# Norms, gating and turning dealt into the seven-product stages, gate rows into routing, skip term begun in the projection

## The reference, cut to what matters

```
layer 0: h = modulate(rms_norm(x)); o = gated_delta(h);
         o = rms_norm(o per head of 128) * silu(h @ w_z);  x += gate * (o @ w_out)
layer 1: y = ssd(h) + d_skip * xs;  y = rms_norm(y * silu(h @ w_z)) @ w_out;  x += gate * y
both:    h = modulate(rms_norm(x)); route each token (softmax, top-k per expert);
         x += gate * experts(h)
then x = rms_norm(x, final_norm_g), and twice:
         m = mixer(rms_norm(x, mix_pre));  x += rms_norm(m, mix_post)
         f = swiglu(rms_norm(x, ffn_pre)); x += rms_norm(f, ffn_post)
```

## Time and profile before

| | us |
|---|---|
| median of 3 runs (4990.16 to 4994.88) | 4993.59 |
| the profiled execution's own time | 4995.03 |
| its span in the profile | 4993.3 |
| PE busy, of the span | 4098.9 (82%) |
| DVE busy | 2111.5 (42%) |
| ACT busy | 806.3 (16%) |
| POOL busy | 444.8 (9%) |
| mean granted clock of PE, share of full speed | 0.912 |

### The profile page before, as it was taken

How to read it: one execution, slowest core, us unless ns; L and a number is a source line. 1 busy time by engine, 2 the same in 40 slices (tenths; PEclk the granted TensorE clock), 3 DMA queues, 4 the chain that set the end, 5 groups by cost and what they waited for, 6 DMA issues and landing times. The chain is left out here.

```text
span 4993.3 us, 71953 instructions
## 1 busy us (share of the span) xinstructions
PE 4098.9 (82%) x30734; PEld 2813.9 (56%) x30734; DVE 2111.5 (42%) x3566; ACT 806.3 (16%) x1757; POOL 444.8 (9%) x486
## 2 busy tenths in 40 slices
PE   4988988876599996998887847775876999797997
PEld 2577658755244444585586622222355887446876
DVE  1655555554422212274474531110334445464445
ACT  1322232200000001152251000000121000151000
POOL 0012002200011110040040001110000000000000
PEclk7999999988799997989898969998987999898999
DMA  4500230002599991100101259999011222112221
GB/s 164 183 21 2 95 126 2 2 18 109 211 385 388 385 378 62 37 15 30 38 1 68 77 224 391 391 393 365 19 51 38 75 78 93 55 68 72 85 80 51
DMA packets 237213, 664.83 MB, mean 133 GB/s; under 512 B 15122, under 2 KB 32479, under 8 KB 236895
## 3 DMA queue, kind: packets, MB, share of 16 engines
q1 hardware_dynamic: 222302, 639.25, 34.0%
q0 software_dynamic: 14592, 20.98, 2.0%
HBM read 637.12 MB, written 23.07 MB: 132 GB/s over the span
## 5 line engine op out<-in xcount | busy, mean ns | idle before, releaser
L603 PE MATMUL bank<-hT_b,weight_ring 128*128 128x384 f32 x1792 | 592.7, 491 | 17.9 <-PEq L178 17.3
L603 PEld LDWEIGHTS bank<-hT_b,weight_ring 128*128 128x128 f32 x1792 | 339.5, 191 | 265.5 <-issue 41.8
L2292 PE MATMUL bank<-weight_ring,xs_b 128*32 128x512 f32 x2640 | 317.9, 634 | 64.5 <-DMA weight_ring<-in_moe_w_up 58.3
L2292 PE MATMUL bank<-weight_ring_extra_b,xs_b 128*32 128x512 f32 x2480 | 278.7, 600 | 29.2 <-DMA weight_ring_extra_b<-in_moe_w_up 29.2
L1477 PE MATMUL bank<-mixed_b,swiglu_sums_b 128*128 128x256 f32 x1056 | 239.5, 384 | 5.8 <-DVE swiglu_sums_b L1524 5.8
L2292 PEld LDWEIGHTS bank<-weight_ring,xs_b 128*32 128x32 f32 x2640 | 84.3, 116 | 272.7 <-issue 184.0
L1477 PEld LDWEIGHTS bank<-mixed_b,swiglu_sums_b 128*128 128x128 f32 x1056 | 203.5, 193 | 34.9 <-issue 6.5
L2360 DVE TENSOR_SCALAR xs_b<-bank,factor_b,mod_b 128x64 f32<-128x64 f32 (+1 forms) x384 | 95.4, 323 | 296.9 <-PE bank L2275 296.9
L2292 PEld LDWEIGHTS bank<-weight_ring_extra_b,xs_b 128*32 128x32 f32 x2480 | 79.2, 110 | 207.0 <-issue 178.5
L2261 POOL DMA_INDIRECT residual<-moe_out_b,slot_row_parts x80 | 123.9, 1549 | 725.8 <-DVE moe_out_b L2374 711.1
L2349 ACT ACTIVATE moe_silu_b<-bank 128x256 f32<-128x256 f32 x80 | 25.5, 383 | 1003.9 <-PE bank L2292 1003.9
(11 more groups left out here) (491 smaller groups left out, 7593.2 us busy)
## 6 DMA issues: line engine op xcount, KB each, us to landing
weight_ring_extra_b<-in_moe_w_down SPq DMA_DIRECT2D x34, 2048.0 KB, 25.5
weight_ring<-in_moe_w_gate SPq DMA_DIRECT2D x66, 1024.0 KB, 16.8
weight_ring<-in_moe_w_up SPq DMA_DIRECT2D x66, 1024.0 KB, 20.2
weight_ring_extra_b<-in_moe_w_gate SPq DMA_DIRECT2D x62, 1024.0 KB, 17.8
weight_ring_extra_b<-in_moe_w_up SPq DMA_DIRECT2D x62, 1024.0 KB, 18.9
weight_ring<-in_moe_w_down SPq DMA_DIRECT2D x30, 2048.0 KB, 23.6
weight_ring<-in_ada_w SPq DMA_DIRECT2D x24, 2048.0 KB, 7.9
weight_ring<-in_ssd_w_in SPq DMA_DIRECT2D x12, 2048.0 KB, 8.0
```

The source lines that it names most:

```text
L603: last = pe.matmul(acc, w[:, k, c * P:(c + 1) * P], hT[:, k, h * half:(h + 1) * half], start=(k == 0), stop=(k == KT - 1))
L2292: last = pe.matmul(in_bank(g)[lanes[c], :], xs[:, e % 2, kt, g * GROUP:(g + 1) * GROUP], w[:, k, :, c * COLS:(c + 1) * COLS], start=(kt == 0),
```

## The change

`gemm_seven` gets two hooks. `heads` deals the head norms, gating, turning and the spreading of the gate rows into the z products (`DeltaHeads` in layer 0, `BlockHeads` in layer 1); `tail` deals what follows an out product into its last units and behind them (`RouteTail`, `JoinTail`, both through `Renorm`). `norm_rows` takes the place of `load_x` + `norm_turn` and works in groups of two rows, each with its own load. `gate_rows`, `norm_turn`, `load_x`, `add_normed`, `final_norm`, `head_norm`, `rms_rows`, `turn_all` and `store` are gone. Buffers `heads_out`, `X`, `mixed`, `hT` live longer, so that rows stay in SBUF: only `x_dram` and `h_dram`, which the expert stage reads, are still written. In layer 1 rows are turned unscaled, and their inverse root comes in the out product's evacuation. The core of it:

```
 gemm_seven, SP:
+    tail.load(sp); ring.feed(sp, loads[-2][2])
+    for g in range(pairs - 1): tail.store(sp, steps, g)
     ring.feed(sp, last_load)
+    tail.store(sp, steps, pairs - 1); tail.end(sp, pairs)
 gemm_seven, PE:
     (unit 0, plain)
+    heads.spread_gate(pe)
+    u == 1: heads.wait_gate(pe)
+    u >= LAG (3): heads.turn(pe, u - LAG, u % 2, (3, 0))     # 8 transposes, banks 3 and 0 of this unit
+    before products 4 and 1: heads.wait_turned(pe, u - LAG, ...)
     (all units done)
+    for g in range(pairs): steps.turn(pe, g, g - 1 if 0 < g < pairs - 1 else None)
+    heads: turn the last three units (after combined of the last but one)
 gemm_seven, ACT:
+    heads.start_scalar(act, 0)            # layer 0: 24 squares of 128 columns with sums
     evacuate unit 0
+    heads.copy_gate(act); heads.start_scalar(act, 1)          # 24 more
     for u in range(1, len(units)):
+        heads.move_on_scalar(act, u - LAG, ...)
+        evacuate(act, u - 1)              # was behind the copy of the first product
+        heads.on_scalar(act, u - 2)       # layer 1: 2 squares of 512 columns
         copy of the first product
+        g = u - u0                        # u0: first unit of the last load
+        g >= 1: pre_square(g - 1), pre_root(g - 1)
+        M and g >= 0: post_square(g), post_root(g)
+        g >= 1: scale_on_scalar(g - 1)
+    for g in range(pairs - 1): move_on_scalar(g)
+    pre_square, pre_root, scale_on_scalar, move_on_scalar (pairs - 1)
 gemm_seven, DVE, for each u:
     combine(u), evacuate(u)
+    heads.on_vector(dve, u - 1)           # layer 0: 2 x 4 ops of 128 columns; layer 1: 2 of 512
+    g >= 1: pre_inverse(g - 1), scale_on_vector(g - 1)
+    M and g >= 0: post_inverse(g), join(g)
+ behind the units: move_on_vector(0 .. pairs - 2), pre_inverse, scale, move (pairs - 1)

+Renorm: a group is two rows of 1024.
+    square: ACT.Square with accum_out, each waits for the one before
+    mean (DVE) -> root (ACT) -> inverse (DVE); row 0 of a group scaled by ACT, row 1 by DVE
+    join: per row scalar_tensor_tensor (times inverse, times gain), then tensor_tensor (X += M)
+    turn: 8 transposes a row into two banks
+    move: bank 0 by ACT, 4 ops of 128 columns; bank 1 by DVE, 4 ops of 128 with a shift,
+          one of 512 without
 norm_rows:
-    load_x: one DMA of all rows, wait; norm_turn over all rows
+    one DMA for each row, a semaphore for each group; ACT: pre_square(g + 1) before scale(g),
+    move(g - 1) behind it; DVE: pre_inverse(g), scale(g), move(g - 1)
 route:
+    PE, behind the turning of the affinities: for each 512 columns of gate rows 4 spreads;
+    ACT copies them, behind Exp
 conv_project, "turn" jobs of the SSD, before the copy:
+    skip: Y[t, pair] = x * d, one tensor_tensor of 128 columns for each of 4 tiles
 ssd_scan:
-    if s < other: dve.tensor_copy(y, ...)
-    else: wait; dve.tensor_tensor(y, y, ..., ADD)
+    if s >= other: wait
+    dve.tensor_tensor(y, y, ..., ADD)
-    vector_ops: x *= skip; y += x          # after each half of the scan
 layer 1 out product, evacuation:
-    add_gated: tmp = part * gate;           X += tmp
+    add_scaled: tmp = part * inverse * gate; X += tmp
 RouteTail: X rows loaded at the start of the out product; per group the rows are stored to
+    x_dram, the normed rows to h_dram; in layer 0 groups 0 and 1 are normed in place, behind
+    the store of the same rows. The turned rows lie in heads_out, which route reads.
```

More of the change, by code:

```diff
@@ L405, in _ @@
         @block.sync
         def _(sp):
[L407 to L450, removed]
+            for g in range(G):
+                for target, source in sources(g):
+                    sp.dma_start(target, source).then_inc(loaded[g], 16)
@@ L454, in _ @@
         def _(act):
[L455 to L459, removed]
+            if gain is not None:
+                for g in range(G):
+                    steps.post_square(act, g)
+                    steps.post_root(act, g)
+            steps.pre_square(act, 0)
@@ L465, in _ @@
[L465 to L480, removed]
+            if gain is not None:
+                dve.wait_ge(gain_loaded, 16)
+                for g in range(G):
+                    steps.post_inverse(dve, g)
+                    steps.join(dve, g)
@@ L482, in _ @@
+            for g in range(G):
+                steps.pre_inverse(dve, g)
+                steps.scale_on_vector(dve, g)
+                if g:
+                    steps.move_on_vector(dve, g - 1)
+            steps.move_on_vector(dve, G - 1)
         @block.tensor
         def _(pe):
[L484 to L496, removed]
@@ L499, in input_parts @@
[L499 to L510, removed]
-            for target, part in parts:
-                sp.dma_start(target, part).then_inc(loaded, 16)
-            sp.wait_ge(loaded, 16 * len(parts))
+            for g in range(G):
+                steps.turn(pe, g, g - 2 if g >= 2 else None)
@@ L1226, in gemm_seven, with rows_ready, tail_bank @@
         first = core.sb(own, "first_product", 2, 1, HN)
+        def rows_ready(engine, g, q):
+            engine.wait_ge(moved, 2 * (u0 + g) + q + 1)
+        def tail_bank(g, q, i):
+            return core.bank[4 * ((u0 + max(g, pairs - 2)) % 2) + 2 * q + i]
+        row_groups = [[tiles[p], tiles[p + pairs]] for p in range(pairs)]
+        steps = tail.steps(core, own, tail_sems, row_groups, rows_ready, tail_bank) if tail else None
+        turns = steps is not None and steps.hT is not None
+        if heads:
+            heads.begin(own, tail_sems, [[tiles[p], tiles[p + pairs]] for _, p in units], [loads[i][0] for i, _ in units],
+                        moved, combined)
         def tokens(i):
@@ L1254, in _ @@
         def _(sp):
+            if tail:
+                tail.load(sp)
+                ring.feed(sp, loads[-2][2])
+                for g in range(pairs - 1):
+                    tail.store(sp, steps, g)
             ring.feed(sp, last_load)
+            if tail:
+                tail.store(sp, steps, pairs - 1)
+                tail.end(sp, pairs)
         @block.tensor
@@ L2807, in first_norm @@
     hT = core.sb(own, "hT", KT, T)
+    groups = [[t, t + 1] for t in range(0, TT, 2)]
     with ExitStack() as inner:
@@ L2914, in ssd_layer @@
+        inv = core.sb(own, "ssd_inverse", TX)
+        gate = core.sb(own, "gate", 1, D)
         yT = core.sb(own, "ssd_yT", SI // P, NX)
[L2915 to L2916 removed]
+        with ExitStack() as sums:
+            heads = BlockHeads(core, sums, inv[:], kept.rearrange("p (t n) -> p t n", t=TX), yT[:], gate[:])
+            gemm_seven(core, hT[:, :, NC:], [[(f"ssd_z{j}", KT)] for j in range(SI // 512)], range(TC, TT),
+                       heads.evacuate, "ssd_z3", block_sums(core, sums), on_scalar=True, heads=heads)
```

795 lines of the change are left out of this document (558 added, 237 removed).

## The result

The changed kernel takes 4732.4 us (median of 4 runs, 4728.4 to 4738.2) against 4993.1 before: a ratio of 0.948, with 95% interval 0.946 to 0.950. The forecast was 4741, with a range of 4700 to 4790. PE is busy 86% of it, ACT 20% (it was 16%), DVE 43%, and the mean granted clock rose from 0.912 to 0.935.

The account below looks back on a forecast made before the run. PE bounds the products; between them PE stands nearly still while a chain runs through one engine at a time. Gains summing to 252.3 us take the profiled 4995.0 to 4742.7, median 4741, range 4700 to 4790.

Parts of the forecast that it names:

- Products with heads: Layers' z products: head norm, gating, turning and gate rows dealt in; 92.4 against 127.4 and 122.0 against 150.6 us.
- Routing tails: Behind the out products of layers 0 and 1: 21.9 against 59.4 and 19.5 against 45.5 us.
- Join tails: Behind ev_out and od_out 18.5 us, gains 17.1 and 17.2; ffn_down 22.3, gain 14.8; the last 17.0, gain 10.4.
- Norms by groups: Norms ahead of layers 0 and 1, and second part: work by row groups gains 7.0 each and 15.4 us.
- Moves with a shift: Moving rows with a shift, not in the trace: taken as 0.37 us on ACT, 0.4 on DVE, per 128 columns.
- Table loads: Layer 1's z tail: one switch on the path, 1.28 us; the skill's drain of about 1.38 was not used.
- The rest at nothing: Everything outside the listed gains, such as the projection carrying the skip term's DVE jobs, was taken to change by nothing.
- the skip term: Two vector stages behind the scans go, 10.7 and 11.2 us; gain 21.9, costing the projection nothing.
- Rival 2: With less idle, products start at 2.4 GHz: eleven entries save 39 us, 4702; chance 0.15.
- Rivals 1, 3 and 4: Tails 5 us longer each, 4796 (0.17); clock taken away, 5085 (0.03); heads hold PE 3 us a unit, 4777 (0.10).

Follow-up runs that it names:

- Undone parts: Four kernels, each the changed one with z stages, tails, three norms, or gate rows and skip term as before: +62.0, +127.4, +27.2, +34.0 us.
- the run with the other order: Changed kernel with tail operations reordered, none added: ACT squares and scales the last pair ahead of moving the pair before it; 4723.1 us.
- the z stages undone: Changed kernel with both layers' z stages as before: Z kept whole, then head norm or gating, turning and gate rows in own stages; 4794.35 us.
- the norms undone: Changed kernel with the three norms ahead of a layer in whole stages again (load, squares, scaling, turning); 4759.6 us.

## Why the prediction was right, and where it was not

- **What bounds it.** Products bound by PE with room beside them, stages between them bound by a chain: both held. Undone parts cost what their stretches had gained.
- **Products with heads** (gain 35.0 and 28.6, measured 37.9 and 31.8). Products of 83.7 and 110.2 us came out as 81.6 and 107.5. The mis-sized term is the transpose: I took 0.17 each from a stretch of turning in which the clock was at 0.56 to 0.58 on average. Inside a product eight take 0.87 us, 0.109 each, which makes 4.2 us in eight units. From the first spread matmul to the next product PE needed 4.5 and 2.7 us, where I had 5.0 and 2.7; squares came at 0.434, not 0.45. The tails (8.7 and 11.8 with their barriers) were 7.9 and 11.3. And 5.8 and 1.4 us of the two gains are the load of X. I had named it, but not priced it apart.
- **Routing tails** (21.9 and 19.5): 21.4 and 20.0. The order in ACT's queue that the forecast wrote out, squares of the last pair behind all moves, is what the run with the other order took apart.
- **Join tails** (18.5, 22.3, 17.0): 19.35, 23.6, 17.0. Followed from ev_out's last product, the joined rows came at 10.1 (10.3 forecast), but the last square ended at 12.25 and not 11.5, since ACT had the moves of the pair before ahead of both squares; and turning two rows took 3.68, where I had 2.75 and 0.65 for the clock. PE is at the lower level while it turns either pair, though the grant is back at 1.00 between them (3644 to 3646).
- **Norms by groups** (7.0 each and 15.4, measured 8.2, 8.9 and 14.8). In layer 1, from the first load's issue at 1791.84, DVE's last move ended at 24.3 us and ACT's at 25.1, where the forecast had 10.9 for the load and 16.1 behind it, 27.0.
- **Moves with a shift,** unknown before, bounded by 0.28 and 0.54: pitch 0.334 on DVE (eight in 2.67) and 0.359 on ACT (eight in 2.87); I had 0.4 and 0.37. Their groups by shape after the change (L541 and L552), and with them the moves without a shift (L543) and the small squares (L1795):

```profile
L543 ACT ACTIVATE hT_b<-bank,cols_b 128x128 f32<-128x128 f32 x64 | 18.1, 369 | 11.6 <-PE bank L530 11.6
L541 ACT ACTIVATE hT_b<-bank,mod_b,factor_b 128x128 f32<-128x128 f32 x48 | 17.1, 479 | 0.0
...
L552 DVE TENSOR_SCALAR hT_b<-bank,factor_b,mod_b 128x128 f32<-128x128 f32 x48 | 15.8, 409 | 2.2 <-PE bank L530 2.2
L1795 ACT ACTIVATE head_squares_b<-heads_out_b 128x128 f32<-128x128 f32 x48 | 14.9, 310 | 8.2 <-PEq L178 6.8
```

  The Trainium skill (ScalarE: Activation LUTs, What ACT_TABLE_LOAD costs) gives 186 ns plus 0.833 ns a column, about 93 more for each pointer operand and an overlap of about 93: an estimate by it is 0.479 us alone and 0.386 in a row for 128 columns with scale and bias. The trace has 0.479 alone and less in a row, 0.359.
- **Table loads.** The switch on the path, ahead of the root in the tail of layer 1's z product, is a load of 1.28 us at 2601.45, with the root at 2602.75; the one in layer 0's is at 1032.18, with the root at 1033.47. The drain that the same section of the Trainium skill adds does not show here either.
- **The rest at nothing.** Right in sum (-1.3), but it is made of parts that cancel: the stages behind the first norms (decays) took 2.2 and 1.2 more at a lower clock, the expert stages 2.3 less and 3.9 more, the two up projections 1.7 and 2.5 less, odd_mix 1.6 less, attention 1.3 more, ev_out's product 1.5 more and od_out's 1.6 less, and an SSD projection 2.2 less (that one stands in the skip term). That the sum is near nothing is luck. Rival 2, that the clock helps by 39 us, did not come: the tails are still mostly idle for PE, and ev_out's product, for one, is at 0.50 in its first 3.05 us. Rivals 1, 3 and 4 have no trace: no tail is 5 us over its forecast, no product lost its clock, no unit with heads stood 3 us.

## What to carry to other kernels

Where one engine bounds the products and chains of stages stand between them, write the chain's operations into the units' slack, and price each against what it lies beside: on the bounding engine it counts in full, elsewhere nothing until the slack is used, and then more than its length where PE stood long enough to come back at the lower clock (16 matmuls in 6.05 instead of 3.62 us here). In a tail written as one stage the order in each in-order queue, SP's among them, is the next bound: begin the last rows' chain before moving the earlier rows, and issue what ends the stage before what a later one wants. Before a useless warm-up, look at the first wait of the stage behind: if another engine's result sets it, a faster start only lengthens the pause. Where no such wait stands first, the start counts: 1.7 and 2.4 us in the two out products with the z stages undone.

## What the runs showed of the hardware that I had not expected

- A 256-column matmul in f32 shows as two records of 0.219 us, at 2.4 GHz; a transpose of 128 by 128 as one of 0.109 at 2.4 GHz and about 0.21 at 1.2 GHz.
- A pause of PE of 1.99 us was followed by matmuls at full pace, one of 3.74 us by the lower level, in the same place of the same stage.
- A stage that no edit touches may differ by several us from run to run: the attention stage took 125.7 us from start to next start with the norms undone and 131.9 after the change, with a granted clock of 0.80 and 0.75. What sets it is open.
